# Second expert table gathered token by token and summed in four column quarters of TensorE

## The reference

```python
for l in range(2):
    x = x + mixed @ w_out[l]
    h2 = rms_norm(x, norm2_g[l])
    scores of h2 @ peer_wq[l] against peer_k1[l], peer_k2[l]  ->  idx[token, 128], gate[token, 128]
    hid = einsum("td,tkd->tk", h2, peer_u[l][idx])            # first table, "up"
    x = x + einsum("tk,tkd->td", gelu(hid) * gate, peer_v[l][idx])   # second table, "down"
return rms_norm(x, final_g)
```

## Time and profile before

| | us |
|---|---|
| median of three runs | 2366.01 (2364.57 to 2373.82) |
| the profiled execution | 2369.01 |
| its span | 2367.2 |
| TensorE, matmuls | 1861.4 (79%) |
| VectorE | 1308.5 (55%) |
| GpSimd | 1128.5 (48%) |
| ScalarE | 510.4 (22%) |
| bytes moved | 774.31 MB, 327 GB/s over the span |

### The profile page before, as it was taken

The page is one execution under the profiler, slowest core; times in us unless marked ns, Lnnn a source line. Parts: engine busy times, 40 slices in busy tenths (PEclk is TensorE's granted clock), DMA queues, the critical chain, the costliest instruction groups (busy, mean ns, idle before and its releaser), DMA issues.

```text
span 2367.2 us, 20979 instructions
## 1 busy us (share of the span) xinstructions
PE 1861.4 (79%) x7072; PEld 1021.4 (43%) x7072; DVE 1308.5 (55%) x3454; ACT 510.4 (22%) x1138; POOL 1128.5 (48%) x1028
## 2 busy tenths in 40 slices
PE   7979988734999986675688897769889777777666
PEld 3449674721448654351245363225546222222222
DVE  2324226589455438759845736774663787444442
ACT  1312113221213213201112321112331112111111
POOL 0000000036542334547765646775664777777774
PEclk9979999857999998796999999999999999999999
DMA  9657775558999999899899999999998999999997
GB/s 342 225 198 242 281 249 198 183 173 304 379 391 366 394 379 343 308 382 348 325 352 371 345 383 376 371 331 374 371 341 301 353 352 352 378 362 358 364 364 272
DMA packets 279275, 774.31 MB, mean 327 GB/s; under 512 B 20353, under 2 KB 65665, under 8 KB 278913
## 3 DMA queue, kind: packets, MB, share of 16 engines
q0 software_dynamic: 147456, 536.94, 61.0%
q1 hardware_dynamic: 131712, 236.04, 27.9%
HBM read 771.85 MB, written 1.05 MB: 327 GB/s over the span
## 4 chain that ended last, share of the span: by engine, by line
PE 44%; DMA 17%; POOL 16%; DVE 13%; issue 7%; ACT 1%; SPq 0%; another core or an unknown queue 0%; ACTq 0%; DVEq 0%; POOLq 0%
POOL arena L1802 16%; DMA arena<-in_peer_v_dram,eidx 13%; PE psum L797 11%; PE psum L435 11%; PE psum L449 10%; PE psum L638 5%; DVE arena L1740 3%; PE psum L656 3%; DMA ring<-in_w_ffn_up_dram 3%; DVE x L1757 1%; DMA arena<-in_peer_u_dram,eidx 1%; PE psum L613 1%; DVE mixs L1594 1%; PE psum L463 1%; DVE smi L1658 1%
## 5 line engine op out<-in xcount | busy, mean ns | idle before, releaser
L797 PE MATMUL psum<-arena,diag 128*128 128x512 f32 x1796 | 947.6, 657 | 380.7 <-DMA arena<-in_peer_v_dram,eidx 336.7
L1802 POOL DMA_INDIRECT arena<-in_peer_u_dram,eidx x512 | 552.4, 1079 | 845.3 <-DVE eidx L1720 489.9
L1740 DVE CUSTOM_DVE_ANT_0 arena<-arena,osb 128x1024 f32<-128x1024 f32 x512 | 622.1, 1221 | 350.8 <-DMA arena<-in_peer_u_dram,eidx 321.0
L1802 POOL DMA_INDIRECT arena<-in_peer_v_dram,eidx x512 | 575.9, 1125 | 374.3 <-PE psum L797 221.4
L797 PEld LDWEIGHTS psum<-arena,diag 128*128 128x128 f32 x1796 | 331.2, 202 | 926.1 <-DMA arena<-in_peer_v_dram,eidx 607.6
L1130 ACT ACTIVATE diag<-const,wexp 128x128 f32<-128x128 f32 x449 | 171.9, 396 | 560.9 <-PE psum L797 363.6
L435 PE MATMUL psum<-ring,hT 128*128 128x512 f32 x560 | 251.9, 600 | 4.2 <-DMA ring<-in_w_in_dram 2.3
L449 PEld LDWEIGHTS psum<-hT,ring 128*128 128x128 f32 x1536 | 178.4, 193 | 21.6 <-issue 19.0
L449 PE MATMUL psum<-hT,ring 128*128 128x128 f32 x1536 | 179.8, 276 | 4.1 <-issue 2.5
L638 PE MATMUL psum<-hT,ring 128*128 128x130 f32 x1408 | 164.2, 279 | 7.5 <-DMA ring<-in_w_ffn_up_dram 6.7
L638 PEld LDWEIGHTS psum<-hT,ring 128*128 128x128 f32 x1408 | 163.2, 195 | 12.5 <-DMA ring<-in_w_ffn_up_dram 8.3
(11 more groups left out here) (318 smaller groups left out, 1347.2 us busy)
## 6 DMA issues: line engine op xcount, KB each, us to landing
ring<-in_w_in_dram SPq DMA_DIRECT2D x84, 1024.0 KB
ring<-in_w_ffn_up_dram SPq DMA_DIRECT2D x44, 1024.0 KB
ring<-in_peer_wq_dram SPq DMA_DIRECT2D x32, 1024.0 KB
ring<-in_w_out_dram SPq DMA_DIRECT2D x24, 1024.0 KB
ring<-in_w_ffn_down_dram SPq DMA_DIRECT2D x20, 1024.0 KB
arena<-in_peer_u_dram,eidx POOLq DMA_INDIRECT x512
arena<-in_peer_v_dram,eidx POOLq DMA_INDIRECT x512
ring<-in_w_mem_kv_dram SPq DMA_DIRECT2D x2, 1024.0 KB
```

Source lines behind the costliest of these rows:

```text
L797: ins = pe.matmul(bank(b), diags(n % 4), arow(i)[:, 512 * h:512 * h + 512], start=(k == 0), stop=(k == 127))
L1740: v.tensor_tensor_reduce(out=arow(i), in0=arow(i), in1=row_y[t], scale=1.0, scalar=0.0, op0=ALU.mult, op1=ALU.add, accum_out=hid[:, c:c + ...
L1802: pool.indirect_dma_start(arow(i), None, tab, bass.IndirectOffsetOnAxis(ap=eidx[:, 128 * t + k:128 * t + k + 1], axis=0)).then_inc(sig.sem ...
```

## The change

The second table is gathered by token instead of by expert: one indirect DMA fetches all 128 experts of one token, experts on the partitions. For that the indices are transposed on TensorE and copied to `eidxT`. A pass now does its 128 ups first, then its 128 downs; `token(k)` gives the token of the k-th down, so that four downs in a row belong to tokens 32 j + k // 4 for j = 0 to 3. Gelu, the gate product, a transpose of the weights and one copy are done once a pass (`weigh`). The copy writes token 32 j + c's weights into column 33 c of quarter j of `spread` (the space of `kv1`, zeroed once after B1's attention), so that each 32-column slice holds one token's weights in one column and zeros in the others. TensorE waits for four gathered rows and does eight matmuls, for each half h of the width one for each quarter j, with 128 rows, 32 columns and 512 moving columns, whose outputs lie in partitions 32 j to 32 j + 31. The diagonals, the VectorE downs and the lag are gone. The paces are divided over 236 gathers. A gather buffer of a down is free when the second half's matmul of its own quarter is done.

```diff
@@ -24,11 +24,7 @@
 SLOT = 4096
 NSLOT = 3
 ROWS = 8
-G = 8
-LAG = 10
...
 ADD = (0, 2)
-SHARE = (1, 2)
...
         wexp = sb("wexp", 256)
-        diag = sb("diag", 4 * 128)
+        eidxT = sb("eidxT", 256, U32)
...
+        spread = kv1[:, :].rearrange("p (j c) -> p j c", j=4)
...
-        def on_vector(n):
-            return n < 128 and n % 128 not in (0, 127) and n % SHARE[1] < SHARE[0]
-
-        def gated_by(n):
-            (l, t), k = ORDER[n // 128], n % 128
-            return l, t, k // 32
+        def token(k):
+            return 32 * (k % 4) + k // 4
...
-            pace, credit = FIRST / (118.0 - LAG), 0.0
+            credit = 0.0
             todo = routing + ahead + ["M01"]
-            for n in range(512 + LAG):
-                if n < 512:
-                    l, t, hh = gated_by(128 * (n // 128) + min(n % 128 + 4, 127))
-                    while not sig.has("gated", l, t, hh):
-                        advance(todo)
-                    gather("up", n)
-                if 0 <= n + AHEAD - LAG < 512:
-                    plan.append(("weigh", n + AHEAD - LAG))
-                if n >= LAG:
-                    gather("down", n - LAG)
-                if n in (128 + LAG, 256 + LAG, 384 + LAG):
-                    todo += ["M%d%d" % ORDER[n // 128 + 1]] if n < 384 else ["F0"]
-                    pace = SECOND / (118.0 - LAG)
-                credit += pace
-                while todo and credit >= 1:
-                    cost = advance(todo)
-                    if cost != "end":
-                        credit -= cost or WAITS
-                credit = min(credit, 1.0)
+            for i, (l, t) in enumerate(ORDER):
+                todo += [(), ("M10",), ("M11",), ("F0",)][i]
+                pace = (SECOND if i else FIRST) / 236.0
+                for g in range(256):
+                    n, k = 128 * i + g % 128, g % 128
+                    if g < 128:
+                        while not sig.has("gated", l, t, min(k + 4, 127) // 32):
+                            advance(todo)
+                        gather("up", n)
+                    else:
+                        while not (sig.has("index", l, t) and sig.has("zeroed")):
+                            advance(todo)
+                        if k == 0:
+                            plan.append(("weigh", i))
+                        gather("down", n)
+                    credit += pace
+                    while todo and credit >= 1:
+                        cost = advance(todo)
+                        if cost != "end":
+                            credit -= cost or WAITS
+                    credit = min(credit, 1.0)
...
+                b = b_[7]
+                w.wait_ge(*at("routed", l, t, 3))
+                wait_bank(b)
+                pe.transpose(bank(b)[:, 0:128], junk[:, 512:640], ident).then_inc(*up("index_turn", s))
+                bank_free[b] = at("index", l, t)
+
+            def weigh(i):
+
+                t, b = ORDER[i][1], ADD[0]
+                w.wait_ge(*at("weight", i))
+                wait_bank(b)
+                pe.transpose(bank(b)[:, 0:128], wexp[:, 128 * t:128 * t + 128], ident).then_inc(*up("weight_turn", i))
+                bank_free[b] = at("spread", i)
...
             def down(n):
-                t, k = ORDER[n // 128][1], n % 128
-                if on_vector(n):
+
+                i, k = n // 128, n % 128
+                if k % 4 != 3:
                     return
-                i = slot_of["down", n]
-                w.wait_ge(sig.sem("row%d" % i), landed_at["down", n])
-                w.wait_ge(*at("diag", n))
+                for j in range(4):
+                    w.wait_ge(sig.sem("row%d" % slot_of["down", n - 3 + j]), landed_at["down", n - 3 + j])
+                w.wait_ge(*at("spread", i))
                 for h in range(2):
                     b = ADD[h]
-                    if k == 0:
+                    if k == 3:
                         wait_bank(b)
-                    ins = pe.matmul(bank(b), diags(n % 4), arow(i)[:, 512 * h:512 * h + 512], start=(k == 0), stop=(k == 127))
-                ins.then_inc(*up("down_mm", n))
+                    for j in range(4):
+                        m = n - 3 + j
+                        ins = pe.matmul(bank(b)[32 * j:32 * j + 32, :], spread[:, j, 32 * (k // 4):32 * (k // 4) + 32],
+                                        arow(slot_of["down", m])[:, 512 * h:512 * h + 512], start=(k == 3), stop=(k == 127))
+                        if h == 1:
+                            ins.then_inc(*up("down_mm%d" % j, m))
                 if k == 127:
                     for h in range(2):
-                        bank_free[ADD[h]] = at("peer_x", n // 128, h)
+                        bank_free[ADD[h]] = at("peer_x", i, h)
...
-            def gelu(n):
-
-                t, k = ORDER[n // 128][1], n % 128
-                if k % G != G - 1:
-                    return
-                c = 128 * t + k + 1 - G
-                w.wait_ge(*at("dot", n))
-                if n >= 256:
-                    w.wait_ge(*at("accumulate", 126))
-                act.activation(wexp[:, c:c + G], hid[:, c:c + G], ACT.Gelu_apprx_tanh).then_inc(*up("gelu", n // G))
-
-            def weigh(n):
-                t, k = ORDER[n // 128][1], n % 128
-                if on_vector(n):
-                    return
-                w.wait_ge(*at("weight", n // G))
-                if n % 4 in diag_held:
-                    w.wait_ge(*at("down_mm", diag_held[n % 4]))
-                diag_held[n % 4] = n
-                c = 128 * t + k
-                act.activation(diags(n % 4), ident, ACT.Copy, scale=wexp[:, c:c + 1]).then_inc(*up("diag", n))
+            def weigh(i):
+
+                (l, t), c = ORDER[i], slice(128 * ORDER[i][1], 128 * ORDER[i][1] + 128)
+                w.wait_ge(*at("dot", 128 * i + 127))
+                act.activation(wexp[:, c], hid[:, c], ACT.Gelu_apprx_tanh).then_inc(*up("gelu", i))
...
                     yield from heads()
+                    w.wait_ge(*at("att_values", s, len(block_units(s, t)) - 1))
+                    v.memset(kv1[:, :], 0.0).then_inc(*up("zeroed"))
...
                     w.wait_ge(*own.now())
-                    if l:
-                        w.wait_ge(sig.sem("row%d" % slot_of.get(("down", 128 * t + 127), 0)), landed_at.get(("down", 128 * t + 127), 16))
-                    v.tensor_tensor(eidx[:, cols_], e1, e2, ALU.add).then_inc(*up("routed", l, t, hh))
+                    v.tensor_tensor(e1, e1, e2, ALU.add).then_inc(*own.up())
+                    w.wait_ge(*own.now())
+                    v.tensor_copy(eidx[:, cols_], e1).then_inc(*up("routed", l, t, hh))
...
                     yield
+                w.wait_ge(*at("index_turn", s))
+                v.tensor_copy(eidxT[:, 128 * t:128 * t + 128], bank(b_[7])[:, 0:128]).then_inc(*up("index", l, t))
...
-                if k % G == G - 1:
-                    we = wexp[:, c + 1 - G:c + 1]
-                    w.wait_ge(*at("gelu", n // G))
-                    w.wait_ge(*at("gated", l, t, k // 32))
-                    v.tensor_tensor(we, we, gate[t][:, k + 1 - G:k + 1], ALU.mult).then_inc(*up("weight", n // G))
+
+            def weigh(i):
+
+                (l, t), c = ORDER[i], slice(128 * ORDER[i][1], 128 * ORDER[i][1] + 128)
+                w.wait_ge(*at("gelu", i))
+                w.wait_ge(*at("gated", l, t, 3))
+                v.tensor_tensor(wexp[:, c], wexp[:, c], gate[t], ALU.mult).then_inc(*up("weight", i))
+                w.wait_ge(*at("weight_turn", i))
+                w.wait_ge(*at("zeroed"))
+                v.tensor_copy(spread[:, :, 0:1024:33], bank(ADD[0])[:, 0:128].rearrange("p (j i) -> p j i", j=4)).then_inc(*up("spread", i))
 
             def down(n):
-                t, k = ORDER[n // 128][1], n % 128
-                i = slot_of["down", n]
-                if on_vector(n):
-                    c = 128 * t + k
-                    w.wait_ge(sig.sem("row%d" % i), landed_at["down", n])
-                    w.wait_ge(*at("weight", n // G))
-                    if n > 2:
-                        w.wait_ge(*at("accumulate", n - 2))
-                    v.scalar_tensor_tensor(x3[:, t, :], arow(i), wexp[:, c:c + 1], x3[:, t, :], ALU.mult,
-                                           ALU.add).then_inc(*up("accumulate", n))
-                elif k == 127:
-                    w.wait_ge(*at("down_mm", n))
-                    if n == 127:
-                        w.wait_ge(*at("accumulate", 126))
+                if n % 128 == 127:
+                    for j in range(4):
+                        w.wait_ge(*at("down_mm%d" % j, n - 3 + j))
                     for h in range(2):
-                        add_to_x(t, h, ADD[h], "peer_x", n // 128, h)
+                        add_to_x(ORDER[n // 128][1], h, ADD[h], "peer_x", n // 128, h)
...
                     w.wait_ge(*at(*held[i]))
-                w.wait_ge(*at("routed", l, t, k // 32))
```

(13 more changed lines are left out.)

10 lines of the change are left out of this document (4 added, 6 removed).

## The result

| kernel | median, us | runs | ratio to the kernel before, 95% interval |
|---|---|---|---|
| before | 2366.2 | 2364.6 to 2373.8 | |
| changed | 2516.6 | 2514.6 to 2521.4 | 1.0636 [1.0608, 1.0664] |

The change made the kernel slower by 150 us. Two repeats of the changed kernel beside later experiments gave 1.0620 [1.0574, 1.0665] and 1.0595 [1.0559, 1.0630].

A forecast was written before the change was run, and what follows sets the result against it. Gather issue, transfer rate and buffers were taken to bound the gathers nearly together, engine work mostly behind them. Terms summed to +48 on the profiled 2369.0 us, less 3.0: 2414, rounded to 2410; range 2280 to 2530.

The forecast's parts named there:

- R3: Rival: the column quarters run one after the other, a down 1.72 us of TensorE; sum +270, 2636 us; chance 0.11.
- Diagonals and gelus, 0: Removed diagonal copies, small gelus and multiplies on ScalarE: off the chain, covered by the transfers, worth 0.
- In the last tile there is nothing but dots: Last tile's first-table gathers: only dots on VectorE, 1.36 us a gather, 174 us for the half.
- The order in the middle and first tiles, +12 and +15: First-table halves: routing lies wholly among dots on VectorE; +12 us in each middle tile, +15 in the first.
- The group's loop, 1.53 us a down: Second-table half: issues, flight, parallel matmuls and hand-back set the loop; 1.53 us a gather, 196 us in the last tile.
- R2: Rival, slower: half clock and buffers give 1.78 us a gather in last tile's downs; 2475 us, 2535 at most; chance 0.18.
- Middle downs, +5: Middle tiles' second-table gathers: next layer's weights fill what gathers leave; +5 us a tile, ends -12 and +25.
- First block, -8, and zeroing, +3: 600 to 900 us: 8 of 22 us of diagonals on the chain regained; zeroing `kv1` costs 3 us of VectorE once.
- Turns and end, +8 and -6: Turns between halves: +2 us a tile, +8; at the end the last group finishes sooner after landing, -6.
- R1: Rival, faster: separated halves give ups 1.25, downs 1.36 us; last tile -34, total about -85, 2285 us; chance 0.27.

The follow-up runs named there:

- E3: Changed kernel plus three unread full matmuls after each group of four downs in the last pass, to raise TensorE's clock; 2503.3 us, 1.0783 to the kernel before.
- E9: Changed kernel with rows taken alone in passes 1 to 3 and paces moving routing steps from ups to downs; 2450.0 us, 1.0321 to the kernel before.
- E7: Changed kernel with each dot product over the first 256 of 1024 columns; 2433.8 us, 1.0264 to the kernel before.
- E8: Changed kernel with rows taken alone in passes 1 to 3, groups of four kept in pass 0; 2473.7 us, 1.0419 to the kernel before.
- E6: Changed kernel with the next pass's first routing quarter forced by down 100; 2518.0 us, 1.0622 to the kernel before.
- E4: Kernel before, diagonals and accumulates kept, with only the order changed to 128 ups, then 128 downs; 2596.2 us, 1.1172 to the kernel before.

## Why the prediction was wrong in size and right in direction

The forecast was +48 us on the profiled execution; it was +146. By pass, with the 2 us of each turn put in: forecast +12, +19, +19, -2, measured +38, +33, +38, +35. The direction and the kinds of cost were right. What failed are the sizes of three terms: the ups of the last pass, taken at 1.36 us a gather, measured 1.60; the group's loop there, taken at 1.53 us, measured 1.694; and the middle passes' downs, taken at +5 us, which took 29 and 24 us more than 128 gathers at the pace of before (440 and 434 us for 256). The first pass's 26 us stay without a cause.

R3, the quarters one after the other, fell: at full clock the eight matmuls of a group take 1.92 us (E3), where 16 serial passes of 0.43 are 6.9. Estimated from the Trainium skill ("TensorE: Matmul & The Clock Gate", Part 3), which has 2.38 times for three column tiles, four would be 3.2 times; here 6.9/1.92 is 3.6.

- **Diagonals and gelus, 0:** right. 521 us less of TensorE's work brought no gain in the whole; their cover was the transfers and the interleaving.
- **"In the last tile there is nothing but dots": this step failed, as a fact and as a price.** I took 1.36 us a gather; it was 1.60. As a fact: three of the four routing quarters of the last tile fell into its ups (line L1716, once a quarter and tile, runs three times in 2082 to 2286); in the kernel before only one conversion came after that pass's first dot, at 2000.6. The conversion of indices, one per quarter and tile, ran until 2229.6, 148 us into the last pass (changed kernel first, then E9; ns min/median/max, first and last start):

```profile
L1716 DVE CAST eidx<-junk x16: 181/181/182, 491.5 to 2229.6; 128x32 uint32<-128x32 f32 x16
```

```profile
L1717 DVE CAST eidx<-junk x16: 181/181/251, 490.7 to 1995.3; 128x32 uint32<-128x32 f32 x16
```

  In the earlier trace rows I had read 60 gathers of routing beside a full VectorE and applied that only to the earlier tiles; I never worked out from the pace where the planner's backlog would stand (256 slots at 340/236 give a pass 369 of the planner's credit, 128 at 340/108 gave it 403). As a price: I had the earlier trace rows, an issue ending 0.81 us after the dot's end, and still priced the issue near 1.24. E9, with the routing out, has ups of 1.42 us (182 us for 128), with GpSimd's issues at 142.6 us for 126, or 1.13 each and 0.30 between two. So 0.18 of my miss of 0.24 is the routing. The other 0.06 is the dots at most, since E9's ups stand at a DMA share of 0.97, and E7's, with short dots, took 1.39 us.
- **The order in the middle and first tiles, +12 and +15:** right where it was worked out. VectorE was above 90% as said, 148.5 of 154 us, and the first 90 gathers of the two middle passes took 153 and 151 us, in the forecast's 147 to 165; the first 69 of the first pass took 124.5, where 128 to 145 was forecast. What the term left out is the rest of the ups: the last 37 gathers took 70 and 77 us, 1.9 and 2.1 each against 1.72 before, at a DMA share of 0.98 and 1.00. The ups took 224 and 230 us in all.
- **The group's loop, 1.53 us a down: mis-sized, as R2 says.** All four terms came out: 3.7 of issues, 6.2 of flight (my 5.2 was the short end), 3.5 of matmuls (2.0 at full clock), 0.2. I took 1.53, within the range for full clock, 1.40 to 1.58, and had in R2 the clock of 0.67 to 0.68 in stretches that were busier than this one. The clock was 0.72. 128 times 0.16 is 21 us in the last pass; the clock's share of it is about E3's 19. With the 31 us of the ups that is more than the 37 by which the last pass was over: its turn and its end were shorter than taken.
- **Middle downs, +5: this step failed too.** They took 249 and 241 us, 1.94 and 1.89 a gather. That weights "fill what the gathers leave" did not hold: the 249 us stand at a DMA share of 0.92, with TensorE at 153 of 248 and a clock of 0.77, and GpSimd waited 95 us for buffers, so the loop held here too. E8 shows that taking the group's wait away there leads into TensorE's own time, at the same price.
- **First block, -8, and zeroing, +3:** the zeroing took 3.5 us, as taken. The -8 did not come: the downs of the first pass stand at a DMA share of 0.92 and 339 GB/s, where the kernel before ran from 600 to 1097 us at 1.00 and 368. Which wait makes them long is not shown.
- **Turns and end, +8 and -6:** the turns were small (1.5 us from the second pass's last dot to the end of the copy) but for the one into the second pass, whose first indices came 28 us late. I had said that the turned indices are ready near gather 90 and had not asked the same of the next tile's first ones. E6 shows that this hole is not a cost by itself.
- **R1** has its mechanism in E9's last pass, 21 us under the kernel before, once the routing is elsewhere and the rows stand alone. The other three passes have no such elsewhere.

The 98 us beyond the forecast: by pass 26, 14, 19, 37 and 2 at the start. Nearest of all the cases was R2 with 2475, and 2535 at most. What stays open: what makes the first pass 38 us longer, how the first three passes' ups divide between VectorE's queue, GpSimd's waits for dots and transfers, and how much the convolution that moved with the pace adds. The last could have been tried with a planner that places it apart, and was not. Nor was an order tried that keeps the quarters and brings the cover back, with the downs of one pass beside the ups of the next where the data allow it.

## What to carry to other kernels

When two kinds of work alternate and each loads another engine, their separation into phases makes each phase as long as its own engine wants, and the engine that is idle in a phase gives nothing back: here the order alone cost 275 us (E4), though every total of busy time stayed below 80%. Before pricing a buffer loop, take the clock and the flight from the stretch with the least work on that engine, not from the cleanest one. And if a queue of steps is paced by slots, count the backlog at the start of every phase before saying what runs in it.
